# Moving the last head's prompt-memory products from the output projection to the boundary before the second feed-forward stage

## The chip, the cores and the metric

The kernel runs on one core of one Trainium2 chip. The metric is the device time of one execution in microseconds, as the median of the runs. A profiled execution has a span (first to last instruction) and a time of its own that is a little longer.

## What is computed

One inference step of a hybrid decoder layer: a half-step feed-forward block, a mixer (four mLSTM heads and a causal convolution side by side, one input and one output projection), and a second half-step feed-forward block, each inside RMSNorms. 256 prompt tokens and 8 x 4 decode tokens go through it together. What the change touches is the new memory of the prompt, one 256 x 256 matrix per head, an output of its own that nothing else in the layer reads:

```
g_keys = jnp.exp(bt[..., -1:] - bt + it - m_new[..., None])
C_new = g_state[..., None, None] * C + jnp.einsum('bhs,bshd,bshe->bhde', g_keys, kc, vc)
...
x = x + rmsnorm(mix, p['g_mix_post'])
x = x + FFN_RES * rmsnorm(swiglu(rmsnorm(x, p['g_ffn2_pre']), p['w_ffn2_gate'], p['w_ffn2_up'],
                                 p['w_ffn2_down']), p['g_ffn2_post'])
```

For the prompt C starts at zero, so the kernel computes it as one product of keys (scaled, `ktg`) and values (`vtok`) over the 256 tokens.

## The kernel before

Weights come as 656 pieces of 128 x 1024 fp32 (512 KB), in the order of use, through four slots. SyncE issues the load of a piece when the slot's low part has been made (`lo_ready`). ScalarE writes the high part `whi` (`split_hi`, L835), VectorE (L1219) or GpSimd (L1737) the low part `wlo`, and TensorE makes three products per block of 128 x 128 weights: high by high, high by low, low by high (`multiply`, L444 to L446; in the convolution's half of the output projection L765 to L767). Each product streams 288 columns, the tokens. An fp32 product, as in the mixer or with `ones`, shows in the profile as two records.

Each engine has one program written out by hand, and runs it in that order; semaphores are the only link. Around the change the order is this.

- **Mixer.** `update_memory(h, b)` (L689 to L706) makes products for head h between the products of the projection, at places set by the table `updates` and `LATE`: b = 0 to 7 for the decode memories, b = 8 for the prompt memory (L704, four products of 256 columns into bank 7). For head 3, b = 8 stands in piece 6 of the first four output tiles (counted from 0). VectorE evicts them: into `C` (L1612), and b = 8 into `cpr` (L1617), with `cu_evicted` counted up by one each, 9 per head. ScalarE then issues the stores `cs_out` (2 MB, L1106) and `cp_out` (256 KB, L1107).
- **Output projection.** 16 tiles. VectorE copies a tile into `y` (L1699), ScalarE squares it, GpSimd sums the squares into `ssq`.
- **Boundary.** `post_norm(1, (4, 5))` (L521 to L532) on TensorE: sums over channels (L516), two idle products of `keep_warm` (L507, 128 x 128 by 128 columns, fp32, into bank 3), a wait for the factor `nfac` from VectorE (L1236), and its broadcast into banks 4 and 5 (L531). Then `keep_warm(6)` (L820). Meanwhile `residual` on VectorE (L1271 to L1306) makes the new `x` by chunks of 128 channels, with banks 6 and 7 as scratch: chunk 0 in bank 6 (`xl`, L1285), chunk 2 as the first in bank 7 (L1298), and each chunk's `xl` (L1240). ScalarE's `x_operands` (L858 to L878) first copies bank 5 to `rpost` (L862), which GpSimd needs for chunk 1, then per chunk writes `xh` (L874) and a square into `y` (L875), with the splits of pieces 4 to 9 of the second feed-forward stage between.
- **Second feed-forward stage.** `project_first` uses pieces 0 to 9 with five tiles at a time, as the chunks come. Tile 5 needs pieces 10 and 11; at its step k = 7 TensorE waits for `xsq_sum` and makes `feature_sums` (L511, L556 to L558). Before it, ScalarE waits for `cs_stored` and `cp_stored` 64 (L1201, L1202), and then its `ffn` (L915) loads a table and splits pieces 10 to 14. VectorE's `residual` ends with the low parts of pieces 9, 10 and 11, then comes `square_tree` (L1320, four additions at L1325, the last of which gives `xsq_sum`), then its own waits for `cs_stored` and `cp_stored`. GpSimd waits for `xsq_sum` and makes the low parts of pieces 12 and 13.

In SBUF the mixer's buffers lie in the room of the feed-forward's `hh`, `hl` and `y`. Before, `qkvo` and `yc` stand behind `ml`, and `rows2`, `bc`, `vtok` and `ktg` reach into the room of `y`, where `ktg` would be overwritten from tile 8 of the output projection on.

Of the kernel before, what the change touches and what calls it, by code (L numbers as in the profile page):

```python
# [29 lines left out]
P = 128  # L30
# [140 lines left out]
def hybrid_layer_kernel(nc, stream, x_in, vecs, gate_vec, c_in, n_in, conv_in,  # L171
                        y_out, cp_out, np_out, cs_out, ns_out, m_out, conv_out):
    with ExitStack() as ctx:
# [3 lines left out]
        def sem(name):  # L177
            return ctx.enter_context(nc.semaphore(name))
# [24 lines left out]
        def place(name, shape, dt=F32, where=None):  # L203
            t = nc.alloc_sbuf_tensor_at(name, shape, dt, offset=where if where is not None else arena[0])
            if where is None:
                arena[0] += -(-4 * int(np.prod(shape[1:])) // 32) * 32
            return t
# [11 lines left out]
        arena[0] = mix_at  # L219
        mh = place("mh", [P, D_MLSTM // P, TOK], F32R)  # L220
        ml = place("ml", [P, D_MLSTM // P, TOK], F32R)
        qkvo = place("qkvo", [P, 4, DC, TOK])
        yc = place("yc", [P, CC, TOK])
        c_at = arena[0]
        C = place("C", [P, NB, DC, DH])
        lfb = place("lfb", [H, PADT], F32, c_at)
# [13 lines left out]
        st = place("st", [P, SEQ + P + NS])  # L240
        col = place("col", [P, 6, H])
        qw = place("qw", [P, DC, 2, NS])
        assert arena[0] <= y_end, (arena, y_end)
        arena[0] = y_end
        gt = place("gt", [H, 5, TOK], F32, arena[0])
# [81 lines left out]
        ln_var, ln_sd, ln_t, ln_sig, ln_silu, ln_hi, conv_ready = (  # L327
            sem("ln_var"), sem("ln_sd"), sem("ln_t"), sem("ln_sig"), sem("ln_silu"), sem("ln_hi"), sem("conv_ready"))
        out0_done = sem("out0_done")
        old_first, y_second, x_first, x_second = (sem("old_first"), sem("y_second"), sem("x_first"),  # L330
                                                  sem("x_second"))
        nn_ready = sem("nn_ready")
# [94 lines left out]
        def _(pe):  # L427
# [90 lines left out]
                if last:  # L518
                    mm.then_inc(norm_sum, 1)

            def post_norm(stage, banks):  # L521

                pe.wait_ge(ssq_added, SQ_BUFS + (XC - 1) * (stage + 1))
                token_sums(ssq, True, False)
                pe.wait_ge(sq_ready, XC * (stage + 1))
                token_sums(sq[:, 1, :], False, True)
                keep_warm(2)
                pe.wait_ge(norm_fac, stage + 1)
                for b in banks:
                    for c, lo in enumerate(BLOCKS):  # L530
                        mm = pe.transpose(bank[b][:, lo:lo + P], nfac[:, c:c + 1].broadcast_to([P, P]), ident[:, :])  # L531
                    mm.then_inc(norm_row, 1)  # L532
# [156 lines left out]
            def update_memory(h, b):  # L689
# [15 lines left out]
                                           vtok[:, t, :], start=(t == 0), stop=(t == 1))  # L705
                mm.then_inc(cu_done, 1)  # L706

            def ln_mean():
                pe.wait_ge(ysum_added, 2 * H)
                pe.matmul(bank[4][:, 0:TOK], ones[:, :], ysum[:, :], start=True, stop=True).then_inc(ln_sum, 1)  # L710
# [8 lines left out]
            def between(p, j):  # L719


                for h in range(H):
                    k = p - KEYS_AT[h]
                    late = LATE[h] > 0
                    if (k, j) == (6, 2):
                        broadcast_rows(h)
                    if (k, j) == (9, 5):
                        to_token_major(h)
                    if (k, j) == (13, 1 if h else 5):
                        scores(h)  # L730
                    if (k, j) == ((16, 1 if h else 4) if late else (14, 1)):
                        query_memory(h)
                    if (k, j) == ((14, 5) if h else (15, 1)):
                        denominators(h)
                    if (k, j) == ((17, 5) if late else (15, 5)):
                        attend(h)
                    b = updates.get((k - LATE[h], j))
                    if b is not None:
                        update_memory(h, b)
                if (p, j) == (MIX_FROM, CH - 1):  # L740
                    pe.wait_ge(xsq_sum, 2)
                    feature_sums()
                if (p, j) == (89, 6):
                    ln_mean()
                if (p, j) == (92, 4):
                    ln_squares()
# [69 lines left out]
                for q in range(4):  # L816
                    out_half(OUT_T + q, OUT_P + 4 + q, True, i)

            post_norm(1, (4, 5))
            keep_warm(6)  # L820
            ffn(FFN2_P, FFN2_T, sum(FF_HALVES), 2 * XC, 3)

            post_norm(2, (4, 5))
# [3 lines left out]
        def _(act):  # L827
# [30 lines left out]
            def x_operands(g, pre, stage, splits):  # L858

                n_new, n_x = (XC - 2) * stage, XC * (stage + 1)  # L860
                act.wait_ge(norm_row, 2 * stage + 2)
                act.activation(rpost[:, :], bank[5][:, 0:TOK], ACT.Copy).then_inc(rpost_ready, 1)  # L862
                for c in range(1, XC):
                    for p in splits:
                        if splits[p] == c:
                            split_hi(g + p)
                    if c == 1:
                        act.wait_ge(x_ready, n_x + 1)
                        act.activation(x[:, 0, :], bank[6][:, 0:TOK], ACT.Copy).then_inc(x_first, 1)
                        act.wait_ge(x_second, stage + 1)  # L870
                        act.wait_ge(x_hi, n_x + 1)
                    else:
                        act.wait_ge(x_new, n_new + c - 1)
                    act.activation(xh[:, c, :], x[:, c, :], ACT.Copy, scale=gain(pre, c)).then_inc(x_hi, 1)  # L874
                    act.activation(y[:, c, :], x[:, c, :], ACT.Square).then_inc(xsq_ready, 1)  # L875
                    if c == 1:
                        act.wait_ge(x_first, stage + 1)
                        act.activation(y[:, 0, :], x[:, 0, :], ACT.Square).then_inc(xsq_ready, 1)  # L878
# [157 lines left out]
            def head_part(h, k):  # L1036
# [65 lines left out]
                        act.wait_ge(ro_ready, 2 * h)  # L1102
                    act.activation(scr[:, 4, :], bank[7][:, 0:TOK], ACT.Abs).then_inc(den_ready, 1)
                if k == 20 + LATE[h]:
                    act.wait_ge(cu_evicted, (NB + 1) * (h + 1))
                    act.dma_start(cs_out[h], C[:, :, :, :]).then_inc(cs_stored, 16)  # L1106
                    act.dma_start(cp_out[h], cpr[:, :, :]).then_inc(cp_stored, 16)  # L1107

            def gate_part(h, o):

# [86 lines left out]
            act.activation(y[:, XC - 1, :], last, ACT.Copy).then_inc(tile_evicted, 1)  # L1197
            post_root(3, 1.0)
            x_operands(FFN2_P, "g_ffn2_pre", 1, NEXT_SPLITS)

            act.wait_ge(cs_stored, 16 * H)  # L1201
            act.wait_ge(cp_stored, 16 * H)  # L1202
# [7 lines left out]
        def _(dve):  # L1210
# [60 lines left out]
            def residual(g, stage, T, post, pre):  # L1271

                n_x, n_t, n_new = XC * (stage + 1), XC * stage, (XC - 2) * stage
                dve.wait_ge(norm_row, 2 * stage + 1)
                t = bank[6][:, 0:TOK]
                dve.scalar_tensor_tensor(out=t, in0=y[:, 0, :], scalar=gain(post, 0), in1=bank[4][:, 0:TOK],
                                         op0=ALU.mult, op1=ALU.mult).then_inc(t_ready, 1)
                dve.wait_ge(t_ready, n_t + 1)
                dve.wait_ge(old_first, stage + 1)
                dve.scalar_tensor_tensor(out=xh[:, 0, :], in0=t, scalar=gain(pre, 0), in1=scr[:, 0, :],  # L1280
                                         op0=ALU.mult, op1=ALU.add).then_inc(x_hi, 1)
                dve.wait_ge(x_hi, n_x + 1)
                dve.tensor_tensor(t, t, x[:, 0, :], ALU.add).then_inc(t_ready, 1)
                dve.wait_ge(t_ready, n_t + 2)
                dve.scalar_tensor_tensor(out=xl[:, 0, :], in0=t, scalar=gain(pre, 0), in1=xh[:, 0, :].bitcast(F32),  # L1285
                                         op0=ALU.mult, op1=ALU.subtract).then_inc(x_ready, 1)
                for m, c in enumerate(range(2, XC)):
                    for p in NEXT_LOW:
                        if NEXT_LOW[p] == c:
                            split_lo(g + p)  # L1290
                    t = bank[7 - m % 2][:, 0:TOK]
                    if m == 1:
                        dve.wait_ge(x_first, stage + 1)
                    if m > 1:
                        dve.wait_ge(x_new, n_new + m - 1)
                    if c == XC - 1:
                        dve.wait_ge(tile_evicted, T)
                    dve.scalar_tensor_tensor(out=t, in0=y[:, c, :], scalar=gain(post, c), in1=bank[4][:, 0:TOK],  # L1298
                                             op0=ALU.mult, op1=ALU.mult).then_inc(t_ready, 1)
                    dve.wait_ge(t_ready, n_t + m + 3)  # L1300
                    dve.tensor_tensor(x[:, c, :], t, x[:, c, :], ALU.add).then_inc(x_new, 1)
                    x_lo(pre, c - 1, n_x)
                x_lo(pre, XC - 1, n_x)
                for p in NEXT_LOW:
                    if NEXT_LOW[p] >= XC:
                        split_lo(g + p)  # L1306
# [230 lines left out]
            def head_part(h, k):  # L1537
# [65 lines left out]
                    link(dve.tensor_tensor(scr[:, 4, :], scr[:, 4, :], bc[:, R_EM:R_EM + TOK], ALU.max))  # L1603
                    dve.reciprocal(scr[:, 4, :], scr[:, 4, :]).then_inc(rden_ready, 1)
                first = k - 16 - LATE[h]
                for b in ((0, 1, 2), (3, 4), (5, 6, 7), (8,))[first] if 0 <= first < 4 else ():
                    dve.wait_ge(cu_done, (NB + 1) * h + b + 1)
                    src = bank[4 if b % 2 else 7][:, :]
                    if b < NB:
# [427 lines left out]
```

## Time and profile before

| | |
|---|---|
| median of 3 runs | 2172.04 us (2172.04 to 2172.37) |
| profiled execution: its own time | 2172.34 us |
| profiled execution: span | 2170.6 us |
| granted TensorE clock, mean | 0.998 |
| TensorE busy | 2156.2 us (99%) |
| VectorE, ScalarE, GpSimd busy | 996.3, 902.2, 962.2 us (46, 42, 44%) |
| DMA, mean over the span | 171 GB/s |

A row of the timeline gives start and duration in us, the engine (PE is TensorE's products, PEld its weight loads, DVE VectorE, ACT ScalarE, POOL GpSimd, ACTq the DMA issues of ScalarE), the line of the kernel, the operation and its tiles, how many, and in brackets how long the engine was idle before and what released it. Products are pipelined: one shows 0.29 us, while the next starts 0.13 us after it.

### The profile page before, as it was taken

The page shows a single profiled execution, that of the slowest core. Times are in us where ns is not written, and L with a number is a line of the kernel's source. Part 1 is how long each engine was busy: PE and PEld are TensorE (multiplying, and loading weights), DVE is VectorE, ACT ScalarE, POOL GpSimd, SP SyncE. Part 2 cuts the span into 40 slices and gives each one's busy share as a digit, 9 for nine tenths or more (in the row PEclk, how much of TensorE's full clock was granted, in tenths as well). Part 3 has the DMA queues.
Part 4 walks back from the last instruction along what each step waited for, and adds up shares of the span by engine and source line. Part 5 has one row for each costly group of instructions (what it writes and reads, how often), then busy time and mean ns, then how long its engine had stood idle before and what let it go on. Part 6 is the DMA issues. An engine that isn't in the chain of part 4 may idle for free.

```text
span 2170.6 us, 41896 instructions
## 1 busy us (share of the span) xinstructions
PE 2156.2 (99%) x16326; PEld 2146.3 (99%) x16326; DVE 996.3 (46%) x1403; ACT 902.2 (42%) x1172; POOL 962.2 (44%) x561
## 2 busy tenths in 40 slices
PE   9999999999999999999999999999999999999997
PEld 9999999999999999999999999999999999999997
DVE  6533332224333225978768737643432223333323
ACT  6433333333433335634345536434343333333343
POOL 1444443344444444566656332444443334444454
PEclk9999999999999999999999999999999999999999
DMA  6454554544454544555646544544455454545453
GB/s 242 164 172 156 170 169 165 166 164 167 162 167 161 173 159 148 202 187 206 220 179 213 188 162 136 180 160 172 164 165 169 161 170 159 170 160 172 157 173 112
DMA packets 101765, 371.39 MB, mean 171 GB/s; under 512 B 11408, under 2 KB 14480, under 8 KB 100656
## 3 DMA queue, kind: packets, MB, share of 16 engines
q1 hardware_dynamic: 97488, 349.78, 48.1%
q10 hardware_dynamic: 4064, 20.33, 2.6%
q8 instruction: 63, 1.03, 0.2%
q14 instruction: 22, 0.18, 0.0%
q0 software_dynamic: 128, 0.07, 0.0%
HBM read 357.06 MB, written 13.07 MB: 171 GB/s over the span
## 4 chain that ended last, share of the span: by engine, by line
PE 96%; DVE 1%; ACT 1%; POOL 1%; issue 1%; DMA 0%; SPq 0%; POOLq 0%; ACTq 0%; DVEq 0%
PE bank L446 30%; PE bank L444 30%; PE bank L445 30%; PE bank L765 1%; PE bank L767 1%; PE bank L766 1%; DVE wlo L1219 0%; ACT whi L835 0%; PE bank L700 0%; POOL wlo L1737 0%; PE bank L704 0%; DMA raw<-stream 0%; PE bank L659 0%; PE bank L641 0%; DVE y L1325 0%
## 5 line engine op out<-in xcount | busy, mean ns | idle before, releaser
L1737 POOL TENSOR_TENSOR wlo<-raw,whi 128x1024 fp32r<-128x1024 f32 x332 | 798.3, 2407 | 881.5 <-ACT whi L835 762.4
L444 PE MATMUL bank<-xh,whi 128*128 128x288 f32 x3585 | 1064.4, 297 | 1.2 <-DVE xl L1240 0.9
L445 PE MATMUL bank<-xl,whi 128*128 128x288 f32 x3585 | 1059.2, 295 | 0.0
L446 PE MATMUL bank<-xh,wlo 128*128 128x288 f32 x3585 | 1057.9, 295 | 0.0
L835 ACT ACTIVATE whi<-raw 128x1024 fp32r<-128x1024 f32 x654 | 689.4, 1056 | 606.5 <-PE bank L446 576.1
L1219 DVE TENSOR_TENSOR wlo<-raw,whi 128x1024 fp32r<-128x1024 f32 x324 | 471.3, 1456 | 774.3 <-ACT whi L835 773.0
L444 PEld LDWEIGHTS bank<-xh,whi 128*128 128x128 f32 x3585 | 676.1, 189 | 4.0 <-DVE xl L1240 2.0
L446 PEld LDWEIGHTS bank<-xh,wlo 128*128 128x128 f32 x3585 | 675.0, 188 | 0.0
L445 PEld LDWEIGHTS bank<-xl,whi 128*128 128x128 f32 x3585 | 674.0, 188 | 0.4
L446 PE MATMUL bank<-hh,wlo 128*128 128x288 f32 x1408 | 417.4, 296 | 0.0
L444 PE MATMUL bank<-hh,whi 128*128 128x288 f32 x1408 | 416.1, 296 | 0.0
L445 PE MATMUL bank<-hl,whi 128*128 128x288 f32 x1408 | 410.5, 292 | 0.0
L445 PEld LDWEIGHTS bank<-hl,whi 128*128 128x128 f32 x1408 | 268.4, 191 | 0.0
L444 PEld LDWEIGHTS bank<-hh,whi 128*128 128x128 f32 x1408 | 264.5, 188 | 0.0
L446 PEld LDWEIGHTS bank<-hh,wlo 128*128 128x128 f32 x1408 | 263.8, 187 | 0.0
L1760 POOL TENSOR_TENSOR scr<-scr 128x288 f32<-128x288 f32 x88 | 74.5, 847 | 207.8 <-ACT scr L924 207.8
L928 ACT ACTIVATE hh<-scr 128x288 f32 (+1 forms) x88 | 39.1, 444 | 274.8 <-DVE scr L1357 274.8
L924 ACT ACTIVATE scr<-scr 128x288 f32<-128x288 f32 x88 | 39.2, 445 | 220.3 <-DVE scr L1336 220.3
L1336 DVE TENSOR_TENSOR scr<-bank,rstd 128x288 f32<-128x288 f32 x176 | 80.3, 456 | 76.1 <-PE bank L446 72.5
L1499 DVE SCALAR_TENSOR_TENSOR bank<-upad,vec,bank 128x256 f32<-128x256 f32 x232 | 92.7, 480 | 0.1
L1750 POOL TENSOR_TENSOR ssq<-ssq,sq 128x288 f32<-128x288 f32 x45 | 36.4, 809 | 81.5 <-ACT sq L976 54.8
L1359 DVE TENSOR_TENSOR hl<-scr,hh 128x288 f32 (+1 forms) x88 | 40.3, 458 | 64.0 <-ACT hh L928 64.0
(260 smaller groups left out, 1089.4 us busy)
## 6 DMA issues: line engine op xcount, KB each, us to landing
raw<-stream SPq DMA_DIRECT2D x656, 512.0 KB, 3.4
C<-c_in ACTq DMA_DIRECT2D x4, 2048.0 KB, 8.9
cs_out<-C ACTq DMA_DIRECT2D x4, 2048.0 KB, 7.6
conv_out<-upad ACTq DMA_DIRECT2D x4, 302.0 KB, 6.5
y_out<-x_res SPq DMA_DIRECT2D x4, 288.0 KB, 2.6
upad<-conv_in ACTq DMA_DIRECT2D x4, 272.0 KB, 3.2
cp_out<-cpr ACTq DMA_DIRECT2D x4, 256.0 KB, 9.1
x_res<-x_in SPq DMA_DIRECT2D x4, 144.0 KB, 5.4
```

What stands on the lines that cost most here:

```text
L444: pe.matmul(out, wh, mov_hi[:, k, :], start=first, stop=False)
L445: pe.matmul(out, wh, mov_lo[:, k, :], start=False, stop=False)
L446: return pe.matmul(out, wl, mov_hi[:, k, :], start=False, stop=last)
L835: act.activation(whi[:, g % SLOTS, :], raw[:, g % SLOTS, :], ACT.Copy).then_inc(hi_ready, 1)
L924: act.activation(scr[:, 2, :], scr[:, f % 2, :], ACT.Sigmoid).then_inc(sig_ready, 1)
L928: act.activation(hh[:, k, :], scr[:, 4, :], ACT.Copy).then_inc(h_hi, 1)
L1219: dve.tensor_tensor(wlo[:, g % SLOTS, :], raw[:, g % SLOTS, :], whi[:, g % SLOTS, :].bitcast(F32), ALU.subtract).then_inc(lo_ready[g % SLO ...
L1336: ins = dve.tensor_tensor(out, src, rstd[:, :], ALU.mult)
L1359: dve.tensor_tensor(hl[:, k, :], scr[:, 4, :], hh[:, k, :].bitcast(F32), ALU.subtract)\
L1499: ins = dve.scalar_tensor_tensor(out=out, in0=up_prompt(j, SEQ, k), scalar=w, in1=acc, op0=ALU.mult, op1=ALU.add)
L1737: pool.tensor_tensor(wlo[:, g % SLOTS, :], raw[:, g % SLOTS, :], whi[:, g % SLOTS, :].bitcast(F32), ALU.subtract).then_inc(lo_ready[g % SL ...
L1760: pool.tensor_tensor(scr[:, 5 + f % 2, :], scr[:, f % 2, :], scr[:, 2, :], ALU.mult)\
```

## The change

The four products of head 3, b = 8, leave the output projection. One of them (256 columns) stands in `post_norm(1, ...)` in place of its two idle products, the other three behind it in place of `keep_warm(6)`; the last one counts up `last_update`. ScalarE evicts them into `cpr` in `x_operands`, behind `rpost`, and counts up `last_state`, for which VectorE waits ahead of its first use of bank 7. ScalarE issues `cp_out` of head 3 behind `x_operands` and ahead of its waits for `cs_stored` and `cp_stored`. VectorE's eviction of them is left out, and the counts of `cu_evicted` for head 3 are one lower. `qkvo` and `yc` are placed in the room of `y`, and what stood behind them moves down into the room of `hh` and `hl`.

```diff
@@ SBUF layout
-        qkvo = place("qkvo", [P, 4, DC, TOK])
-        yc = place("yc", [P, CC, TOK])
         c_at = arena[0]
...
         qw = place("qw", [P, DC, 2, NS])
+        assert arena[0] <= y_at, (arena, y_at)
+        arena[0] = y_at
+        qkvo = place("qkvo", [P, 4, DC, TOK])
+        yc = place("yc", [P, CC, TOK])
@@ TensorE
-            def post_norm(stage, banks):
+            def post_norm(stage, banks, fill=None):
...
-                keep_warm(2)
+                if fill is None:
+                    keep_warm(2)
+                else:
+                    fill((0,))
                 pe.wait_ge(norm_fac, stage + 1)
...
+            def update_last(products):
+
+                for n in products:
+                    c, t = divmod(n, 2)
+                    mm = pe.matmul(bank[7][:, c * DH:(c + 1) * DH], ktg[:, t, c * P:(c + 1) * P], vtok[:, t, :],
+                                   start=(t == 0), stop=(t == 1))
+                if n == 3:
+                    mm.then_inc(last_update, 1)
...
-                    if b is not None:
+                    if b is not None and h * (NB + 1) + b < H * (NB + 1) - 1:
                         update_memory(h, b)
...
-            post_norm(1, (4, 5))
-            keep_warm(6)
+            pe.wait_ge(cu_evicted, H * (NB + 1) - 1)
+            post_norm(1, (4, 5), update_last)
+            update_last((1, 2, 3))
             ffn(FFN2_P, FFN2_T, sum(FF_HALVES), 2 * XC, 3)
@@ ScalarE, x_operands
                 act.activation(rpost[:, :], bank[5][:, 0:TOK], ACT.Copy).then_inc(rpost_ready, 1)
+                if stage:
+                    act.wait_ge(cp_stored, 16 * (H - 1))
+                    act.wait_ge(last_update, 1)
+                    act.activation(cpr[:, :, :].rearrange("p c e -> p (c e)"), bank[7][:, :], ACT.Copy)\
+                       .then_inc(last_state, 1)
@@ ScalarE, head_part
-                    act.wait_ge(cu_evicted, (NB + 1) * (h + 1))
+                    act.wait_ge(cu_evicted, (NB + 1) * (h + 1) - (h == H - 1))
                     act.dma_start(cs_out[h], C[:, :, :, :]).then_inc(cs_stored, 16)
-                    act.dma_start(cp_out[h], cpr[:, :, :]).then_inc(cp_stored, 16)
+                    if h < H - 1:
+                        act.dma_start(cp_out[h], cpr[:, :, :]).then_inc(cp_stored, 16)
@@ ScalarE, ahead of the second stage
             x_operands(FFN2_P, "g_ffn2_pre", 1, NEXT_SPLITS)
+            act.wait_ge(last_state, 1)
+            act.dma_start(cp_out[H - 1], cpr[:, :, :]).then_inc(cp_stored, 16)
 
             act.wait_ge(cs_stored, 16 * H)
             act.wait_ge(cp_stored, 16 * H)
@@ VectorE, residual and head_part
                     t = bank[7 - m % 2][:, 0:TOK]
+                    if m == 0 and stage:
+                        dve.wait_ge(last_state, 1)
...
-                for b in ((0, 1, 2), (3, 4), (5, 6, 7), (8,))[first] if 0 <= first < 4 else ():
+                for b in ((0, 1, 2), (3, 4), (5, 6, 7), (8,) if h < H - 1 else ())[first] if 0 <= first < 4 else ():
```

## Rows read from the trace of the kernel before

**Rows 1.** The page's busy time of each engine.

```profile
PE 2156.2 (99%) x16326; PEld 2146.3 (99%) x16326; DVE 996.3 (46%) x1403; ACT 902.2 (42%) x1172; POOL 962.2 (44%) x561
```

**Rows 2.** Waits of TensorE, whole span: total us, times, longest.

```profile
PE bank L507 <- POOL ident L1803: 1.6, 1, 1.6
PE bank L444 <- DVE xl L1240: 0.9, 2, 0.6
```

**Rows 3.** Timeline in the output projection, around head 3's prompt memory.

```profile
1229.29 0.29 PE L765 MATMUL bank<-xh,whi 128*128 128x288 f32 x1
...
1229.55 0.29 PE L767 MATMUL bank<-xh,wlo 128*128 128x288 f32 x1
...
1229.68 1.89 PE L704 MATMUL bank<-vtok,ktg 128*128 128x256 f32 x8
...
1231.55 0.30 PE L766 MATMUL bank<-xh,whi 128*128 128x288 f32 x1
...
1231.61 0.69 DVE L1617 COPY cpr<-bank 128x512 f32<-128x512 f32 x1 [1.03 <-PE bank L704]
```

**Rows 4.** Timeline of the boundary before the second feed-forward stage.

```profile
1314.89 0.69 PE L507 MATMUL bank<-ones 128*128 128x128 f32 x4
...
1315.59 0.63 PEld L531 LDWEIGHTS bank<-ident,nfac 128*128 128x128 f32 x6 [0.20 <-DVE nfac L1236]
...
1316.30 1.50 PE L507 MATMUL bank<-ones 128*128 128x128 f32 x12
...
1318.22 0.52 DVE L1298 SCALAR_TENSOR_TENSOR bank<-y,vec,bank 128x288 f32<-128x288 f32 x1
...
1318.34 0.41 ACT L869 ACTIVATE x_res<-bank 128x288 f32<-128x288 f32 x1 [1.43 <-DVE xl L1285]
...
1319.27 0.52 DVE L1240 SCALAR_TENSOR_TENSOR xl<-x_res,vec,xh 128x288 fp32r<-128x288 f32 x1
...
1319.84 0.19 PEld L444 LDWEIGHTS bank<-xh,whi 128*128 128x128 f32 x1 [0.30 <-DVE xl L1240]
```

**Rows 5.** ScalarE's copy of one bank, L1087: duration ns minimum/median/maximum.

```profile
L1087 ACT ACTIVATE vtok<-bank x4: 577/580/602, 922.4 to 1187.0; 128x512 f32<-128x512 f32 x4
```

**Rows 6.** Timelines of ScalarE, VectorE and TensorE around the square sum.

```profile
1343.44 0.54 ACT L874 ACTIVATE xh<-x_res,vec 128x288 fp32r<-128x288 f32 x1 [0.51 <-DVE x_res L1301]
...
1344.31 2.00 ACT L835 ACTIVATE whi<-raw 128x1024 fp32r<-128x1024 f32 x2
...
1344.45 3.49 DVE L1219 TENSOR_TENSOR wlo<-raw,whi 128x1024 fp32r<-128x1024 f32 x3
1347.85 5.23 DVE L1325 TENSOR_TENSOR y<-y 128x2304 f32<-128x2304 f32 x4
...
1353.14 0.19 PEld L511 LDWEIGHTS bank<-y,ones 128*128 128x128 f32 x1 [0.19 <-DVE y L1325]
```

**Rows 7.** Timeline of ScalarE where head 3's stores are issued.

```profile
1234.07 1.06 ACT L835 ACTIVATE whi<-raw 128x1024 fp32r<-128x1024 f32 x1 [3.85 <-PE bank L767]
1234.09 0.34 ACTq L1106 DMA_DIRECT2D cs_out<-C  x1
1234.46 0.46 ACTq L1107 DMA_DIRECT2D cp_out<-cpr  x1
```

**Rows 8.** Issue to landing: `cp_out` L1107, `y_out` L413, weight pieces, `conv_out` at 1144.6.

```profile
DMA to landing us min/median/max: 7.4/9.1/10.8
...
DMA to landing us min/median/max: 2.1/2.4/2.8
...
raw<-stream SPq DMA_DIRECT2D x656, 512.0 KB, 3.4
...
conv_out<-upad ACTq DMA_DIRECT2D x1, 302.0 KB, 4.6
```

**Rows 9.** Windows of 1 us at the end: busy time, PEclk, DMA share, GB/s.

```profile
2159.00:2160.00 1.00, 0.54 (x5) 0.30 (x3) 0.75 (x1) 0.41 (x1) 0.00 (x0) 1.00 0.00 0
...
2162.00:2163.00 1.00, 0.00 (x0) 0.00 (x0) 0.96 (x2) 0.00 (x0) 1.00 (x2) 0.79 0.45 171
```

More of the change, by code:

```diff
@@ L329, in hybrid_layer_kernel @@
         out0_done = sem("out0_done")
+        last_update, last_state = sem("last_update"), sem("last_state")
         old_first, y_second, x_first, x_second = (sem("old_first"), sem("y_second"), sem("x_first"),
```

## Prediction

> **What bounds the kernel now.** I read the page first: TensorE is busy for 2156.2 of the span's 2170.6 us [rows 1]. Then the waits of TensorE over the whole span: its two longest are 1.6 us for the constants at the very start and 0.9 us in all, in two places, for `xl` [rows 2]. So nearly all of the time is the issue of products, one per 0.13 us (two steps of the stream are 1229.55 - 1229.29 = 0.26, [rows 3]), and two questions are left: how much product time does the change take out, and what does it make TensorE wait for. For that I read three stretches of the timeline: the last memory product of head 3 [rows 3], the boundary between the output projection and the second feed-forward stage [rows 4], and the end of the boundary, where operands of the second stage are ready and the square sum is due [rows 6]. Last come the issue and landing times of transfers [rows 7, 8] and the granted clock after TensorE stops [rows 9].
>
> **What the change takes out.** In the output projection, `update_memory(3, 8)` issues four fp32 products of 256 columns (8 records). The product before them begins at 1229.55, and the second product behind them at 1231.55: 2.00 us, where two steps of the stream take 0.26 to 0.27 [rows 3]. They cost 2.00 - 0.27 = 1.73 us. TensorE has no wait there, and none follows in the stage [rows 2], so all of the **1.73 us** comes off. VectorE's copy of `cpr` (0.69 us, [rows 3]) goes too; it waited for the product itself, and the split behind it was fed by ScalarE, so this is worth nothing. `cs_out` may be issued one count earlier (35 in place of 36), up to 2 us; nobody waits for it until the second stage: nothing. The new addresses change no instruction, size or wait: nothing, though no row can exclude some tenths.
>
> **The products in their new place.** Before the row of factors there stood two idle products (4 records, from 1314.89, 0.69 us long), and behind it six (12 records, from 1316.30, 1.50 us) [rows 4]. Now one product of 256 columns stands in place of two of 128, and three in place of six: the columns are the same. By the rows: 8 records of 256 columns take 1.73 us, that is 0.43 each product, against (1.50 - 0.275)/11 = 0.11 per record of 128 columns, 0.22 per idle product, 0.45 per two. Cover: the first lies beside the wait for `nfac`, which ended 0.20 us after the weights could have gone in; the three lie beside VectorE's first chunk. Their cost is **0** (between -0.05 and +0.05). The added wait for `cu_evicted` 35 ahead of `post_norm(1)` was met more than 80 us before, since the 36th is the copy at 1231.61 [rows 3]: 0.
>
> **ScalarE and VectorE at the start of the boundary.** ScalarE now waits for `last_update` behind `rpost`, and evicts 512 columns of bank 7; its next instructions and VectorE's chunk 2 (bank 7 is its scratch, new wait for `last_state`) are queued behind. In [rows 3] VectorE's copy began 1231.61 - 1229.68 = 1.93 us after the first record of four products; with three, two records less at 1.73/8 = 0.216, it is 1.50. From 1316.30 this gives 1317.80. The same form on ScalarE took 0.58 us [rows 5], so it ends at 1318.38. ScalarE's next instruction, the copy of `x_res` for chunk 0, waited until 1318.34 in any case [rows 4]: not late. GpSimd's `x_res`, which feeds ScalarE's chunk 1, hangs on `rpost` alone and isn't touched. VectorE's scratch product began at 1318.22 and now begins at about 1318.42: 0.20 late, and with it the `xl` of 1319.27, for which TensorE already waited 0.30 us [rows 4]. So TensorE starts chunk 1 **0.20 us** later (0 to 0.5, if the eviction comes later). Behind that TensorE has no other wait for `xl` in this stage (the second of the two in [rows 2] is in the first stage), and a chunk of it takes 15 products, 2.0 us, so no later chunk becomes short by 0.20. This 0.20 is not added below: it is a part of the next delay.
>
> **The transfer in front of the second stage.** This is the term that decides. `cp_out` for head 3 was issued at 1234.46, 85 us ahead of the wait for `cp_stored` [rows 7]. Now it is issued by ScalarE at the end of `x_operands`, and the very next statements wait for its landing (`cp_stored` 64), ahead of `ffn`, which begins with the splits `whi` of pieces 10 to 14. Queued behind the wait: those splits. Who waits for them: VectorE's `wlo` of pieces 10 and 11, which stand in program order ahead of the square tree, hence `xsq_sum`, hence TensorE's `feature_sums` in tile 5, which already waits 0.19 us for the tree, and GpSimd's pieces 12 and 13 [rows 6]. There is no slack in that chain: the three splits and the tree run on VectorE without a gap from 1344.45, and TensorE takes the result at 1353.14.
>
> Step by step. ScalarE's last step of `x_operands` is released at 1343.44 [rows 6]; a DMA issue that stands behind an instruction goes out soon after that is released, not after its end: `cs_out` at 1234.09 behind a split of 1.06 us that began at 1234.07 [rows 7]. So the issue is at about 1343.5 plus the 0.20 from above, 1343.7. With a landing time L, ScalarE goes on at 1343.7 + L; 0.1 for the table activation; `whi` of piece 10 takes 1.04 (half of 2.00 and the overlap of two), a handover of 0.03, then VectorE does `wlo` 10 and 11 at 1.13 each ((1347.85 - 1344.45)/3, [rows 6]). The tree begins at 1343.7 + L + 3.43, where it began at 1347.85: it is late by **L - 0.72**, and TensorE with it, since it takes the tree at once. Behind it everything (`pre_root`, `rstd`, GpSimd's splits, evictions) hangs on the tree or on TensorE and shifts alike, so nothing is given back and nothing is added.
>
> L isn't in the trace for this transfer alone: the four `cp_out` took 7.4 to 10.8 us, but behind a `cs_out` of 2 MB issued 0.37 us ahead on the same queue [rows 7, 8]. The nearest rows: `y_out` of 288 KB and up, alone, 2.1 to 2.8; the pieces of 512 KB, 3.4; `conv_out` of 302 KB, beside the weight stream and without a 2 MB transfer, 4.6 [rows 8]. Here 256 KB run beside the stream. I take **3.3**, near the piece, as a smaller transfer that shares the engines with one; the ends are 2.1 and 4.6, and 10.8 for the rival. The stall is then 3.3 - 0.72 = 2.6 us (1.4 to 3.9).
>
> The Trainium skill (DMA: Bandwidth & Descriptors, section on the anatomy of one DMA) fits a transfer issued by GpSimd as 2.0 us fixed plus its bytes over 436 GB/s. By that, as an estimate, 256 KB would land in 2.6 us and the change would cost 0.1 to 0.2 us in all; no row here shows this transfer alone.
>
> **The sum.** -1.73 + (3.3 - 0.72) = **+0.85 us**. On the profiled execution's own time of 2172.34 (span 2170.6 and 1.7 around it) that is 2173.2; the median of the runs, 2172.04, lies 0.3 lower, so the forecast is 2172.04 + 0.85 = 2172.9. With L = 2.1 it is -0.35 (2171.7), with 4.6 +2.15 (2174.2). What a measurement of this kernel can tell from no change is about 0.2%, 4.3 us: the forecast is no change.
>
> **Rivals.**
> Hidden transfer: `cp_stored` would have to be there when ScalarE comes to it, or the tree have slack. Then only the 0.20 us of the start remains: -1.73 + 0.20 = -1.5, 2170.5. Against it stands the order of the statements and the tree without a gap [rows 6]; for it, only that the trace can't show a wait that isn't there yet. 8%.
> Long landing (the slower side): `cp_out` lands as late as it did before, 7.4 to 10.8 us [rows 8]. Its place is ScalarE's wait ahead of `ffn`. The sum is L - 2.45: +5.0 to +8.4, 2177.0 to 2180.4. It is slower than before by over 0.2% from L = 4.3 + 2.45 = 6.8 us. For it: the only rows of this very transfer. Against it: in those 2 MB stood ahead of it, and `cs_out` of head 3 is issued 109 us before and long landed. 6%.
> Clock: TensorE is idle for the stall. At the end of the kernel its last product ends at 2159.54, and the granted clock, 1.00 until 2162, is 0.79 on the mean of the microsecond after [rows 9]: it fell from 2.4 to 1.2 GHz 0.42 us before 2163, about 3.0 us after TensorE stopped. A stall of 2.6 us is near that, and one of 3.9 is over it, though then some of it lies at piece 10 and splits in two. Each microsecond at 1.2 GHz costs 0.5. No row shows how long it would stay there under work; for 8 us, as long as from that fall to the end of the span, it would be 4.0 more, 2176.9, and I hold 1 to 2 for more likely. The Trainium skill (TensorE: Matmul & The Clock Gate, section on why this matters) warns of idle gaps between bursts of products for the same reason. 8%, half of it below +4.3.
> That the products don't fill the place they are put in (they come late for `last_update`) is in the 0 to 0.5 of the start and is swallowed by the later delay, as long as that is larger.
>
> **How the numbers follow.** Forecast with L between 2.1 and 4.6: 77%. Hidden 8%, long landing 6%, clock 8%, something unseen that gains over 4.3 us 1%. The range reaches from the hidden case, 2170.4, to the upper end of L with a clock loss of 1.4: 2174.2 + 1.4 = 2175.6. Within 0.2%: 77 + 8 + 4 = 89%; slower 6 + 4 = 10%; faster 1%.
>
> **What would show it.** In the profile after: no record of `vtok,ktg` at 1229 and the stage shorter by 1.7; 8 such records around the factors; VectorE's first bank 7 product 0.2 later; an idle time of ScalarE in front of the `whi` of piece 10 that ends with the landing of `cp_out`, and an idle time of TensorE at `feature_sums` of L - 0.7, released by the tree; granted clock 1.00 through it. The forecast is wrong if ScalarE issues the transfer only after its queue has run dry (then 0.5 more), if L leaves 2.1 to 4.6, or if the tree turns out not to be what `feature_sums` waits for.

## The result and the profile after

The changed kernel takes 2176.51 us in the median against 2172.06 of the kernel before: a ratio of 1.0019 with a 95% interval of 1.0012 to 1.0027, that is **+4.45 us (+0.20%)**. Its executions scatter from 2173.69 to 2178.90 (one more, of 4285.91, was disturbed and is left out), where those of the kernel before lie between 2171.86 and 2172.37. The forecast was 2172.9 with a range of 2170.4 to 2175.6: the time lies outside of it.

The profiled execution took 2176.27 us with a span of 2174.5, 3.9 more than the span before. The waits of TensorE over the whole span (total us, times, longest), which answer to [rows 2], show where to look:

```profile
PE bank L514 <- DVE y L1351: 2.8, 1, 2.8
PE bank L510 <- POOL ident L1829: 1.6, 1, 1.6
PE bank L447 <- DVE wlo L1243: 1.5, 1, 1.5
PE bank L447 <- DVE xl L1264: 0.7, 2, 0.4
```

Two waits are new: 2.8 us for the square tree (L514 is `feature_sums`) and 1.5 for a low part. First the boundary, where the products stand now. The timeline, to be read beside [rows 3, 4] (L718 is `update_last`, L882 ScalarE's eviction):

```profile
1312.48 0.68 PE L718 MATMUL bank<-vtok,ktg 128*128 128x256 f32 x2
...
1313.18 0.63 PEld L537 LDWEIGHTS bank<-ident,nfac 128*128 128x128 f32 x6 [0.43 <-DVE nfac L1260]
...
1313.89 1.46 PE L718 MATMUL bank<-vtok,ktg 128*128 128x256 f32 x6
...
1315.45 0.60 ACT L882 ACTIVATE cpr<-bank 128x512 f32<-128x512 f32 x1 [0.95 <-PE bank L718]
...
1316.08 0.52 DVE L1324 SCALAR_TENSOR_TENSOR bank<-y,vec,bank 128x288 f32<-128x288 f32 x1 [0.19 <-ACT cpr L882]
...
1317.58 0.19 PEld L447 LDWEIGHTS bank<-xh,whi 128*128 128x128 f32 x1 [0.49 <-DVE xl L1264]
```

The factor row begins at 1313.18, where it began at 1315.59: 2.41 us earlier. The same row of the first boundary, which no edit touches, began at 847.74 before and at 847.05 now, so 0.68 of these come from the start of this execution, and 2.41 - 0.68 = 1.73 are the four products. The eviction begins 1.56 us after the three products (expected 1.50), VectorE's first use of bank 7 waits 0.19 (0.20), and the weight load of chunk 1 waits 0.49 in place of 0.30.

Now the stretch that answers to [rows 6], of SyncE, ScalarE, VectorE and TensorE:

```profile
1340.39 0.33 SPq L409 DMA_DIRECT2D raw<-stream  x1
...
1341.18 0.54 ACT L895 ACTIVATE xh<-x_res,vec 128x288 fp32r<-128x288 f32 x1 [0.51 <-DVE x_res L1327]
1341.19 0.34 ACTq L1223 DMA_DIRECT2D cp_out<-cpr  x1
...
1346.82 0.20 ACT L855 ACTIVATE warm<-ones 128x1 f32<-128x1 f32 x1 [4.77 <-DMA cp_out<-cpr]
1346.92 3.89 ACT L851 ACTIVATE whi<-raw 128x1024 fp32r<-128x1024 f32 x4
...
1342.19 1.22 DVE L1243 TENSOR_TENSOR wlo<-raw,whi 128x1024 fp32r<-128x1024 f32 x1
1348.00 2.36 DVE L1243 TENSOR_TENSOR wlo<-raw,whi 128x1024 fp32r<-128x1024 f32 x2 [4.59 <-ACT whi L851]
1350.28 5.23 DVE L1351 TENSOR_TENSOR y<-y 128x2304 f32<-128x2304 f32 x4
...
1349.28 0.40 PE L447 MATMUL bank<-xh,whi 128*128 128x288 f32 x1 [1.53 <-DVE wlo L1243]
...
1355.56 0.75 PE L514 MATMUL bank<-y,ones 128*128 128x288 f32 x2 [2.82 <-DVE y L1351]
```

ScalarE issues the store beside the instruction released at 1341.18 and stands idle until it lands. The issues by line, with size and time to landing, give it:

```profile
cp_out<-cpr ACTq DMA_DIRECT2D x1, 256.0 KB, 5.5
```

VectorE then waits for `whi` of piece 10, and the tree begins at 1350.28. Against 1347.85 and with the 2.41 of the boundary it is 1350.28 - (1347.85 - 2.41) = 4.84 us late, and `feature_sums` with it: 1355.56 - (1353.14 - 2.41) = 4.83. TensorE idles 1.53 us for piece 10 and 2.82 for the tree.

The last part stands behind the wait. Here are windows of 1 us (busy time of the engines; the granted clock, PEclk, is third from the end) and four products of that time, which answer to [rows 9]:

```profile
1355.00:1356.00 1.00, 0.44 (x3) 0.39 (x3) 0.47 (x2) 0.00 (x0) 0.42 (x1) 1.00 0.00 0
1356.00:1357.00 1.00, 1.00 (x8) 0.95 (x7) 0.02 (x1) 0.64 (x2) 1.00 (x1) 0.91 0.00 0
1357.00:1358.00 1.00, 1.00 (x6) 1.00 (x6) 1.00 (x1) 1.00 (x1) 1.00 (x2) 0.50 0.00 0
...
1360.00:1361.00 1.00, 1.00 (x9) 1.00 (x8) 1.00 (x1) 0.00 (x0) 0.27 (x1) 0.89 0.65 254
```

```profile
1356.67 0.32 PE L448 MATMUL bank<-xl,whi 128*128 128x288 f32 x1
...
1357.27 0.44 PE L448 MATMUL bank<-xl,whi 128*128 128x288 f32 x1
1357.51 0.44 PE L449 MATMUL bank<-xh,wlo 128*128 128x288 f32 x1
...
1360.15 0.34 PE L448 MATMUL bank<-xl,whi 128*128 128x288 f32 x1
```

The granted clock falls from 1.00 to 0.50 (2.4 to 1.2 GHz) 1.3 us after TensorE has work again, and is back some 3.4 us later. From 1356.67 to 1360.15 there are 15 steps in 3.48 us, 0.24 for most, where 15 x 0.133 = 2.00 is usual: **1.48 us**. The whole rest of the span says the same: from `feature_sums` to the end it takes 2174.5 - 1355.56 = 818.9 us, against 2170.6 - 1353.14 = 817.5 before.

So the span is accounted for: -0.68 (start) - 1.73 (products) + 4.84 (tree late) + 1.48 (clock) = +3.91, measured +3.9. Without the start, which differs between executions, it is +4.59 against the +4.45 of the medians.

### The profile page after: what moved, and what is told of

It is laid out like the page before. It is cut to its first block, busy times and chain, and to the rows that moved or that the text cites. A ratio compares the mean times of both kernels' runs of the same rounds, so it can differ in the third digit from the quotient of the medians.

```text
span 2174.5 us, 41865 instructions
## 1 busy us (share of the span) xinstructions
PE 2156.0 (99%) x16310; PEld 2145.7 (99%) x16310; DVE 996.1 (46%) x1402; ACT 902.8 (42%) x1173; POOL 963.4 (44%) x561
## 4 chain that ended last, share of the span: by engine, by line
PE 94%; DVE 2%; ACT 1%; POOL 1%; issue 1%; DMA 1%; SPq 0%; POOLq 0%; ACTq 0%; DVEq 0%
PE bank L449 30%; PE bank L447 30%; PE bank L448 30%; PE bank L780 1%; PE bank L782 1%; PE bank L781 1%; DVE wlo L1243 1%; ACT whi L851 1%; DVE y L1351 0%; PE bank L706 0%; POOL wlo L1763 0%; PE bank L665 0%; DMA cp_out<-cpr 0%; DMA raw<-stream 0%; PE bank L647 0%
```

## The experiments

Three theories are told apart. Theory W is the one of the prediction with the clock added: ScalarE's wait for the landing costs the time, through the tree. Theory P lays it on the products and the eviction in the boundary, theory T on the late transfer as such.

### The wait, the place and the transfer

`e1_no_act_wait`: ScalarE doesn't wait for the store. VectorE alone writes where `cpr` lies, and keeps its wait.

```diff
             act.dma_start(cp_out[H - 1], cpr[:, :, :]).then_inc(cp_stored, 16)
 
             act.wait_ge(cs_stored, 16 * H)
-            act.wait_ge(cp_stored, 16 * H)
```

> The changed kernel, with ScalarE's wait for the landing of the stores of cpr ahead of the second feed-forward stage left out (VectorE, which alone writes where cpr lies, keeps its own behind the square tree); the transfer is issued at the same place. Theory W (ScalarE's wait for the landing holds the splits of pieces 10 and 11, these the square tree, this TensorE): the stall and the fall of the clock go, 1.73 us of products stay saved and 0.2 us is lost at chunk 1: 2170.5 us, no idle time of TensorE over 0.6 us behind the start, granted clock 1.00. Rival T (the late transfer itself takes time from the weight stream): about as the changed kernel, 2175 to 2177. Rival P (products and eviction in the boundary cost the time): 2175 to 2177 too, with the loss between the factors and chunk 2.

Measured: 2170.54 us, ratio 0.9993 (0.9984 to 1.0002), scatter 2170.16 to 2171.14. Waits of TensorE between 1300 and 1400 us, and the store:

```profile
PE bank L447 <- DVE xl L1263: 0.2, 1, 0.2
```

```profile
cp_out<-cpr ACTq DMA_DIRECT2D x1, 256.0 KB, 4.4
```

The transfer is issued at the same place and lands after 4.4 us, but nothing is held up by it: T and P fall, W stands. Both new waits are gone. The scatter is gone too, so it came from the wait or from the clock behind it.

`e2_store_early`: both waits stay, and the store is issued ahead of chunk 3.

```diff
                 for c in range(1, XC):
+                    if c == 3 and stage:
+                        act.wait_ge(last_state, 1)
+                        act.dma_start(cp_out[H - 1], cpr[:, :, :]).then_inc(cp_stored, 16)
...
-            act.wait_ge(last_state, 1)
-            act.dma_start(cp_out[H - 1], cpr[:, :, :]).then_inc(cp_stored, 16)
```

> The changed kernel, with both waits left as they are, but the store of cpr issued by ScalarE ahead of chunk 3, some 20 us earlier. W: landed long before ScalarE comes to its wait; 2170.5 us, as the kernel without the wait. T: if a transfer beside the stream costs time it costs it here as well, at chunks 3 to 6: over 2172. P: 2175 to 2177.

Measured: 2170.57 us, 0.9994 (0.9985 to 1.0003). The store was issued at 1317.56 and landed after:

```profile
cp_out<-cpr ACTq DMA_DIRECT2D x1, 256.0 KB, 2.0
```

With the store at another place the rest of the change keeps its gain. The same 256 KB need 2.0 us there and 5.5 at the late place.

`e3_late_store_alone`: the kernel before, with only the store of head 3 moved.

```diff
-                    act.dma_start(cp_out[h], cpr[:, :, :]).then_inc(cp_stored, 16)
+                    if h < H - 1:
+                        act.dma_start(cp_out[h], cpr[:, :, :]).then_inc(cp_stored, 16)
...
             x_operands(FFN2_P, "g_ffn2_pre", 1, NEXT_SPLITS)
+            act.dma_start(cp_out[H - 1], cpr[:, :, :]).then_inc(cp_stored, 16)
```

> The kernel before (products, eviction and idle products where they were), and only the store of head 3's cpr is issued behind x_operands, right ahead of the waits. W: the tree is late by the landing time less 0.9 us; with the 5.5 us that the changed kernel showed that is 4.6, and 1.5 for the clock: 2172.1 + 6.1 = 2178.2 (2176 to 2180, by landing time). P: no product is moved, so 2172.1. T: over 2172.1 too; the run without the wait tells it from W.

Measured: 2176.22 us, 1.0019 (1.0010 to 1.0028): +4.1, less than the +6.1 expected, since the store landed after 3.7 us in the profile, not 5.5. ScalarE's idle time, TensorE's, and a window behind it:

```profile
1346.98 0.20 ACT L839 ACTIVATE warm<-ones 128x1 f32<-128x1 f32 x1 [2.94 <-DMA cp_out<-cpr]
...
1355.72 0.82 PE L511 MATMUL bank<-y,ones 128*128 128x288 f32 x2 [2.82 <-DVE y L1327]
...
1357.00:1358.00 1.00, 1.00 (x6) 1.00 (x5) 0.79 (x1) 0.98 (x2) 1.00 (x1) 0.50 0.00 0
```

The wait alone, with no product moved, makes a kernel slower by about as much as the whole change does: 3.7 - 0.9 = 2.8 us of idle time in one piece, and the clock falls behind it too.

### The two parts that should be cheap

`e5_products_left_out`: the kernel before, without head 3's prompt-memory products and eviction.

```diff
-                    if b is not None:
+                    if b is not None and h * (NB + 1) + b < H * (NB + 1) - 1:
                         update_memory(h, b)
...
```

> The kernel before, with the four products of head 3's prompt memory and their eviction left out altogether (its output then holds head 2's), boundary with its idle products as before. It measures the gain by itself: 1.73 us by the two start times around the products, so 2172.1 - 1.7 = 2170.4. If a wait behind them took the gain (a piece not split in time), it would be nearer to 2172.1. Against the kernel without ScalarE's wait, 2170.54, it gives the price of the products' new place: 0.1 to 0.2 us.

Measured: 2170.40 us, 0.9992 (0.9983 to 1.0001): -1.72. The kernel's output for head 3 is wrong, since its products are left out. The gain is as worked out from two start times. The new place costs 2170.54 - 2170.40 = 0.14 us, which is hardly more than the scatter of the two (2169.96 to 2170.67 here, 2170.16 to 2171.14 in `e1_no_act_wait`).

`e6_layout_alone`: the new placement of the buffers alone.

```diff
-        qkvo = place("qkvo", [P, 4, DC, TOK])
-        yc = place("yc", [P, CC, TOK])
...
+        arena[0] = y_at
+        qkvo = place("qkvo", [P, 4, DC, TOK])
+        yc = place("yc", [P, CC, TOK])
```

> The kernel before with the new SBUF layout alone. All theories: 2172.1, within 0.3. If addresses cost or gave anything, it shows here.

Measured: 2172.00 us, 0.9999 (0.9990 to 1.0008): nothing.

### The clock

`e4_fill_stall`: idle products on TensorE ahead of the wait for the tree.

```diff
                             if k == 7:
+                                if sums == 3:
+                                    keep_warm(12, bank[7])
                                 pe.wait_ge(xsq_sum, sums)
```

> The changed kernel with 12 idle products (2.6 us) on TensorE ahead of its wait for the square sum of the second feed-forward stage, where it idles 2.8 us. If the granted clock falls because of that idle time (with the 1.5 us at piece 10 ahead of it), it stays at 1.00 behind the square sum and 1.5 us come back: 2175.0. If the clock falls for the wait at piece 10, or for another reason, it falls all the same and the time is 2176.5 or more. P and T say nothing of it.

Measured: 2174.71 us, 1.0013 (1.0004 to 1.0022), 1.8 less than the changed kernel; 0.3 of it is the landing time, 5.2 us in this profile. TensorE, and a window:

```profile
1352.35 2.84 PE L510 MATMUL bank<-ones 128*128 128x128 f32 x24
...
1355.34 0.75 PE L514 MATMUL bank<-y,ones 128*128 128x288 f32 x2 [0.15 <-DVE y L1353]
...
1357.00:1358.00 1.00, 1.00 (x10) 1.00 (x9) 1.00 (x1) 0.99 (x2) 1.00 (x2) 1.00 0.00 0
```

The tree comes nearly as late as in the changed kernel (`feature_sums` at 1355.34 against 1355.56), the wait of 1.2 us at piece 10 is there, but the clock stays at 1.00. From `feature_sums` to the end of the span of 2172.8 it takes 817.5 us again. So it is the idle time ahead of the tree that brings the clock down. The executions still scatter over 3.5 us (2173.51 to 2176.99, against 5.2 in the changed kernel), so the clock isn't the main source of the scatter, as far as one profile with the clock at 1.00 tells.

The Trainium skill (TensorE: Matmul & The Clock Gate, section on why this matters) advises against idle gaps between bursts of products. This trace agrees, with 1.48 us lost behind 2.82 us of idle time.

### Why the landing takes so long there

`e7_half_store_late` and `e9_16kb_late`: the store in two parts, one ahead of chunk 3 as in `e2_store_early`, the other at the late place: 128 KB, or 16 KB.

```diff
+            act.dma_start(cp_out[H - 1][:, 1:2, :], cpr[:, 1:2, :]).then_inc(cp_stored, 16)
...
+            act.dma_start(cp_out[H - 1][:, :, DH - 16:DH], cpr[:, :, DH - 16:DH]).then_inc(cp_stored, 16)
```

> The changed kernel, with the store of cpr in two halves of 128 KB: one ahead of chunk 3, the other at the late place; the waits ask for both. The stall is the landing time of the late half less 0.72. If the landing time is long because the transfer shares the engines with the weight pieces (2.0 us ahead of chunk 3, 3.7 to 5.5 late), half the bytes land some 0.5 to 1.5 us earlier: 2174 to 2175.5. If it is a fixed part that is long at that place, the time stays at 2176 or more.

> The changed kernel with 240 KB of cpr stored ahead of chunk 3 and only the last 16 KB (64 bytes of each row) at the late place; the waits ask for both. With 256 KB late the landing took 5.5 us, with 128 KB 5.0. If the rest is time in which the transfer stands behind or beside the piece of 512 KB that SyncE issued 0.8 us ahead of it, 16 KB still land after 4.3 to 4.7 us: stall 3.8, 2174.5 to 2175.5 by the clock. If the transfer's own size made it long, 16 KB land in about 2 us, as 256 KB did ahead of chunk 3: stall 1.3, clock 1.00, 2171.8.

Measured: 2175.85 us, 1.0016 (1.0007 to 1.0025), with a landing time of 5.0 us; and 2175.26 us, 1.0015 (1.0006 to 1.0024), with 4.6. ScalarE's idle time in the two:

```profile
1346.63 0.20 ACT L855 ACTIVATE warm<-ones 128x1 f32<-128x1 f32 x1 [4.25 <-DMA cp_out<-cpr]
```

```profile
1346.27 0.20 ACT L855 ACTIVATE warm<-ones 128x1 f32<-128x1 f32 x1 [3.81 <-DMA cp_out<-cpr]
```

A sixteenth of the bytes saves 0.9 of 5.5 us: the transfer's own size isn't what makes it long. (The half store alone wouldn't have shown it: its time lies between the two ranges that were expected.)

`e10_behind_the_piece`: ScalarE issues the store only when weight piece 12 has landed.

```diff
             act.wait_ge(last_state, 1)
+            act.wait_ge(landed[(FFN2_P + 12) % SLOTS], 16 * ((FFN2_P + 12) // SLOTS + 1))
             act.dma_start(cp_out[H - 1], cpr[:, :, :]).then_inc(cp_stored, 16)
```

> The changed kernel with ScalarE waiting for the landing of piece 12 ahead of the issue of the late store (all 256 KB). If the piece ahead makes the landing long, it is 2.0 to 3.5 us from issue now, though piece 13 is issued beside it; the issue itself comes 4 to 5 us later, so the stall grows by what the wait for the piece is longer than the time saved: 2177 to 2179. If the landing stays at 5 us or more, the piece ahead isn't the cause, and the time is 2180 or more.

Measured: 2177.22 us, 1.0024 (1.0015 to 1.0034). The store's issue, the end of ScalarE's wait, and its time to landing:

```profile
1346.83 0.34 ACTq L1224 DMA_DIRECT2D cp_out<-cpr  x1
1349.11 0.20 ACT L855 ACTIVATE warm<-ones 128x1 f32<-128x1 f32 x1 [6.03 <-DMA cp_out<-cpr]
...
DMA to landing us min/median/max: 2.2/2.2/2.2
```

All 256 KB land in 2.2 us once the piece is through. At the late place, SyncE had issued a piece of 512 KB 0.8 us ahead of the store (1340.39 against 1341.19). But that piece is itself long there: it took 5.7 us to land beside the store, 5.3 in this kernel with the store behind it, and 4.6 with the store 23 us earlier, where it took 3.0 in the kernel before and 3.8 in `e3_late_store_alone`. So something else delays it too, and the traces' DMA packets point to it. The rows give packets, MB and their share of the time of 16 engines. First come, for the changed kernel from 1341.2 to 1347, the queue of the late store (q10) and a queue of the kind `instruction` (q8); then, for the store of 16 KB in `e9_16kb_late`, the packets that began from 1343 to 1344.5 and from 1344.5 to 1346.2:

```profile
q10 hardware_dynamic: 144, 0.26, 11.7%
q8 instruction: 1, 0.02, 2.0%
```

```profile
q10 hardware_dynamic: 255, 0.02, 11.3%
...
q10 hardware_dynamic: 17, 0.00, 0.7%
```

The one packet of q8 (16 KB, by its name a load of instructions) began at 1342.05. It took 2.0% of the 5.8 us of 16 engines, that is about 1.9 us of one. Of the 272 packets of the 16 KB store, fifteen sixteenths had begun by 1344.0; the last sixteenth began from 1345.54 on, and the landing waits for all. The store of the changed kernel looks alike: 135 of its 144 packets had begun by 1344.43, the last 9 from 1345.63 on. So one sixteenth of the store, as if of one engine, came late in both. In the eight profiles in which the packet of q8 ran while the piece's packets moved, the piece took 4.6 to 5.7 us; in the four in which it had ended before (the kernel before, `e3`, `e5`, `e6`), 3.0 to 3.8.

`e3_late_store_alone` thus has a piece 0.8 us ahead of the store, but no such packet in the way, and its store took 3.7 us. Read so, about 1.6 of the 5.5 us are the piece (3.7 against 2.0 and 2.2) and 1.8 the instruction packet (5.5 against 3.7). This is read from kernels that differ in other things too: no run moved that packet by itself, and the profile doesn't number the engines. `e10_behind_the_piece` can't tell the two apart, since by its late issue at 1346.83 both were through.

This run adds one thing on the clock. Its idle time lies in one piece too, but at piece 10, and the clock had fallen before it was over:

```profile
1350.00:1351.00 1.00, 0.00 (x0) 0.00 (x0) 0.71 (x1) 1.00 (x2) 0.00 (x0) 0.90 0.00 0
...
1351.57 0.61 PE L447 MATMUL bank<-xh,whi 128*128 128x288 f32 x1 [2.81 <-DVE wlo L1244]
```

It stood at 0.50 from 1350.8 to 1357.6, while TensorE had the tree to wait for anyway. `feature_sums` came at 1357.86 after a wait of 0.15 us, and the rest of the span of 2175.3 takes 817.4 us: the low clock cost nothing there.

`e8_changed_again`: the changed kernel, a second profile.

> The changed kernel itself, a second profile. W: the idle time of ScalarE ahead of piece 10 follows the landing time of cp_out of this execution, TensorE takes the square sum that much later, and the time differs from the first profile's 2176.27 by the difference of the two landing times, where the clock falls in both.

Measured: 2176.61 us, landing time 5.5, `feature_sums` after 2.83 us of idle time, clock at 0.50 behind it. It is the same picture as at 2176.27, so it holds twice, but it tells nothing of the scatter between 2173.7 and 2178.9.

## Why the prediction was wrong, point by point

- **The products taken out** (-1.73): right. The stage is 1.73 shorter, and without the products at all the kernel gains 1.72.
- **The new place** (0, and 0.20 at chunk 1): right. VectorE waits 0.19 us, the loss is 0.14 by the medians. The layout is worth nothing.
- **The chain from the landing to TensorE** (L - 0.72, no slack, nothing given back): right. With L = 5.5 it gives 4.78, measured 4.84. The issue stood 0.01 us behind the released instruction, nearly as taken. But the stall isn't all at `feature_sums`: with L = 3.7 (`e3`) TensorE idles 2.82 us there and nowhere else, with 4.6, 5.0 and 5.5 it is 2.82 or 2.83 again, and the rest (0.59, 1.01, 1.53) lies at piece 10. Once piece 10 is late too, the idle time ahead of the tree no longer grows with L. The prediction puts the old issue of the store 85 us ahead of the wait; by its rows it was 109 (1234.46 to 1343.4), which changes nothing.
- **The size of L: wrong, and the larger of the two errors.** It was put at 3.3 with an upper end of 4.6; it was 5.5, and 4.4 to 5.5 in the other kernels that issue all 256 KB at this moment with these products moved. The range was taken from stores and pieces of a like size, and the rows of this very transfer (7.4 to 10.8) were set aside because 2 MB stood ahead of it on its own queue. "Beside the stream" stood in the prediction, but what was in flight at that moment wasn't read: a weight piece of 512 KB, issued 0.8 us ahead on SyncE's queue, and the packet of the `instruction` queue on one of the engines. With the piece alone ahead of it (`e3`) the store took 3.7, only 0.4 more than was forecast; the other 1.8 go with the instruction packet. This term gave +2.2 us more than the sum had.
- **The clock: wrongly kept out of the sum.** It stood there as a rival of 8%, with the remark that a stall of 2.6 us is near the 3.0 of [rows 9]. It fell with 2.81 to 2.83 us of idle time in one piece in every profile that has it (the changed kernel twice, `e3`, `e7`, `e9`, `e10`). It cost 1.48 us in the one worked out above, and 1.5 in the other four with the idle time at the tree, by the time from `feature_sums` to the end (819.0 us in each, against 817.5). "1 to 2" was the right price and 8% the wrong chance. A microsecond at 1.2 GHz cost less than the 0.5 of the prediction: 1.48 in 3.4 us, since a step took 0.24 us and not twice 0.133. Even the forecast's own L would have left 2.6 us of idle time; whether the clock falls there no run shows.
- **The sum**: +0.85 + 2.2 + 1.5 = +4.6, the +4.45 measured within the scatter. The way of the delay was right; what failed are two terms, the size of L and the clock's loss, which was put at nothing in the sum. As the change was measured, it stands at the edge of what a measurement can tell from none: +0.20%, with an interval of 0.12 to 0.27%.

The version that keeps the gain is at hand: with ScalarE's wait left out, or with the store issued ahead of chunk 3, the kernel takes 2170.5 us in both cases. That is 1.6 less than before and 6 less than the changed kernel. Its interval against the kernel before just includes 1, though no execution of the two overlaps (up to 2171.14 in both cases, from 2171.47 before).

## What to carry to other kernels

When a store is moved to just ahead of a wait for it, the price is its landing time. Here that was set less by its own bytes than by what was in flight when it was issued, whatever queue that came from: look up that moment in the trace, `instruction` packets included. Follow what is queued behind the waiting instruction until something has no slack; here an output of 256 KB that nobody needs held up the splits, a sum and all products. And when a sum ends in an idle time of TensorE like the one here, put the fall of its clock into the sum, not beside it, unless TensorE has another wait behind it that takes the loss up, as in `e10_behind_the_piece`.

## What the runs showed of the hardware that was not expected

The landing time of one store of 256 KB, issued by ScalarE, was 2.0 us, 2.2, 3.7, 4.4, 5.2 and 5.5, by what was in flight at its moment; 16 KB took 4.6 at the late place. One packet of 16 KB of the kind `instruction`, 1.9 us long, goes with a landing that is 1.8 us later, for a transfer on another queue.

The granted clock can fall after the idle time has ended: in the changed kernel TensorE had been at work again for 1.3 us (from 1355.56) when it went to 1.2 GHz, and it stayed there for 3.4 us of full work. In the other four profiles with 2.82 or 2.83 us of idle time at the tree it fell 0.2 to 0.8 us after TensorE was at work again, and in `e10_behind_the_piece` 0.8 us before it was.
